# Three edits to the RWKV stage of a fused transformer kernel: V's projection in one run ahead of the scan, a shorter last level of a triangular inverse, and row factors computed earlier

## The reference, cut to what matters

```python
xr = h + hh * mu[0]   # and xw, xk, xv, xa, xg: six mixtures of h and its predecessor
r = xr @ w_r
w = -jax.nn.softplus(-(w0 + jnp.tanh(xw @ w1) @ w2)) - 0.5
k = xk @ w_k
v = xv @ w_v
a = jax.nn.sigmoid(a0 + (xa @ a1) @ a2)
g = jax.nn.sigmoid(xg @ g1) @ g2
kk = k * k_k, normalised per head
k = k * (1.0 + (a - 1.0) * k_a)
def step(state, inp):                      # 256 steps, 16 heads of 64
    sa = jnp.einsum('bhvk,bhk->bhv', state, a_t)          # a_t = -kk
    state = state * w_t + sa * b_t + v_t * k_t            # b_t = kk * a
    y_t = jnp.einsum('bhvk,bhk->bhv', state, r_t)
y = group norm of y, + sum(r * k * r_k) * v, times g, then @ w_o
```

## Time and profile before

| | |
|---|---|
| median of 3 runs | 1463.24 us |
| the profiled execution: its own time, its span | 1461.14 us, 1459.3 us |
| granted TensorE clock, mean over the span | 0.992 |
| busy: TensorE, weight loads, VectorE, ScalarE, GpSimd | 95%, 81%, 61%, 49%, 10% |
| chain that ended last, by engine | TensorE 79%, VectorE 8%, ScalarE 4%, issue 3%, GpSimd 2%, DMA 2% |
| the RWKV layer's projections R to V, start to end | 704.51 to 780.27 us |
| scan, first pass and second pass, start of each | 780.75 and 836.67 us |
| scan's end | 895.61 us |

### The profile page before, as it was taken

How to read it: one execution, slowest core, us unless ns; L and a number is a source line. 1 busy time by engine, 2 the same in 40 slices (tenths; PEclk the granted TensorE clock), 3 DMA queues, 4 the chain that set the end, 5 groups by cost and what they waited for, 6 DMA issues and landing times.

```text
span 1459.3 us, 25739 instructions
## 1 busy us (share of the span) xinstructions
PE 1393.1 (95%) x10574; PEld 1177.2 (81%) x10574; DVE 888.2 (61%) x1230; ACT 720.6 (49%) x988; POOL 144.0 (10%) x143
## 2 busy tenths in 40 slices
PE   8999999999999999999898988999999988899998
PEld 8966988987997998885576767799997765699997
DVE  5665655557476655566957677565456666455553
ACT  5455644446545544445555334454444665354442
POOL 0162011100000101100100102000000223000000
PEclk9999999999999999999999999999999999999999
DMA  8733665555646476555454001456474632165462
GB/s 298 234 108 102 199 201 179 168 187 171 216 147 206 159 220 189 190 170 169 146 141 160 4 4 34 155 179 203 147 236 150 209 104 58 57 217 185 142 222 89
DMA packets 86589, 231.93 MB, mean 159 GB/s; under 512 B 15926, under 2 KB 21702, under 8 KB 86346
## 3 DMA queue, kind: packets, MB, share of 16 engines
q1 hardware_dynamic: 85912, 228.17, 49.1%
q0 software_dynamic: 560, 2.11, 0.4%
HBM read 228.14 MB, written 1.08 MB: 157 GB/s over the span
## 4 chain that ended last, share of the span: by engine, by line
PE 79%; DVE 8%; ACT 4%; issue 3%; POOL 2%; DMA 2%; SPq 0%; DVEq 0%; ACTq 0%; POOLq 0%
PE PS L441 48%; PE PS L444 28%; PE PS L456 3%; ACT SH L413 1%; DVE SL L419 1%; POOL AB L818 1%; DVE AB L792 1%; DVE SL L416 1%; DMA ST<-in_rw_w_o 1%; DMA ST<-in_rw_w_v 0%; POOL SM L886 0%; ACT XH L604 0%; DMA ST<-in_w_ple_gate 0%; DVE X L707 0%; ACT JK L589 0%
## 5 line engine op out<-in xcount | busy, mean ns | idle before, releaser
L419 DVE SCALAR_TENSOR_TENSOR SL<-ST,SM,SH 128x1024 fp32r<-128x1024 f32 (+1 forms) x256 | 315.1, 1249 | 168.9 <-ACT SH L413 128.4
L413 ACT ACTIVATE SH<-ST,SM 128x1024 fp32r<-128x1024 f32 (+1 forms) x256 | 282.4, 1122 | 198.6 <-PE PS L444 124.7
L441 PE MATMUL PS<-XH,SH 128*128 128x256 f32 x1224 | 344.2, 281 | 1.5 <-DVE XL L605 1.5
L444 PE MATMUL PS<-XH,SL 128*128 128x256 f32 x1224 | 344.4, 281 | 0.0
L441 PE MATMUL PS<-XL,SH 128*128 128x256 f32 x1224 | 343.5, 281 | 0.0
L416 DVE TENSOR_TENSOR SL<-ST,SH 128x1024 fp32r<-128x1024 f32 (+1 forms) x153 | 196.6, 1299 | 152.3 <-ACT SH L413 126.4
L441 PE MATMUL PS<-SH,XH 128*128 128x512 f32 x544 | 222.6, 409 | 12.9 <-DVE SM L807 2.6
L441 PEld LDWEIGHTS PS<-XH,SH 128*128 128x128 f32 x1224 | 231.3, 189 | 2.9 <-ACT SH L413 1.7
L413 ACT ACTIVATE SH<-ST 128x1024 fp32r<-128x1024 f32 (+1 forms) x153 | 158.5, 1051 | 147.4 <-PE PS L444 123.9
L441 PEld LDWEIGHTS PS<-XL,SH 128*128 128x128 f32 x1224 | 229.1, 187 | 0.9
L444 PEld LDWEIGHTS PS<-XH,SL 128*128 128x128 f32 x1224 | 229.2, 187 | 0.2
(11 more groups left out here) (317 smaller groups left out, 1458.1 us busy)
## 6 DMA issues: line engine op xcount, KB each, us to landing
ST<-in_ffn_w_gu SPq DMA_DIRECT2D x80, 512.0 KB, 4.7
ST<-in_w_mlp_up SPq DMA_DIRECT2D x64, 512.0 KB, 4.7
ST<-in_w_mlp_down SPq DMA_DIRECT2D x64, 512.0 KB, 4.4
ST<-in_ffn_w_down SPq DMA_DIRECT2D x44, 512.0 KB, 4.3
ST<-in_w_attn_in SPq DMA_DIRECT2D x24, 512.0 KB, 4.9
ST<-in_w_conv_in SPq DMA_DIRECT2D x24, 512.0 KB, 4.5
ST<-in_w_ple_gate SPq DMA_DIRECT2D x16, 512.0 KB, 4.3
ST<-in_kv_w SPq DMA_DIRECT2D x16, 512.0 KB, 4.2
```

What stands on the lines that cost most here:

```text
L413: a = ac.do(lambda e: e.activation(h[p0:p1, 0:cols], t[p0:p1, 0:cols], ACT.Copy, scale=sc), ready, t_gt, pe_done.get(i - NSPLIT))
L419: b = ve.do(lambda e: e.scalar_tensor_tensor(l[p0:p1, 0:cols], t[p0:p1, 0:cols], sc, h[p0:p1, 0:cols].bitcast(F32), ALU.mult, ALU.subtract ...
L441: pe.go(lambda e: e.matmul(o, l, r, start=start, stop=stop, skip_group_check=skip))
L444: return pe.do(lambda e: e.matmul(o, l, r, start=start, stop=stop, skip_group_check=skip))
```

## The change

1. The list of units: the two units of the gate's first factor (g1), one unit of V, the gate's second factor (g2, g2t), and then the other seven of V; before, four of V stood ahead of g1, two between g1 and g2, two behind.
2. The order around R: the decay's `low_rank_out` stands ahead of `mix(3)`; the wait for all four banks ahead of R's first unit is gone (`kind_a` waits bank by bank); the terms from a stand behind R's sixth unit, the triangular sums between its sixth and seventh. The products with R (TT, KN, RN) stand behind the gate's first factor. The four strided reads of PE_ stand right behind the writes that they wait for.
3. Lanes 0 and 1 take banks 4 to 7 and lanes 2 and 3 banks 0 to 3; VN is evacuated half by ScalarE, half by VectorE; the products that read V stand in a part of their own, `inputs`, behind the inverse.
4. The last level of the inverse writes only what it changes: eight products of 64 x 32 into the corner of the transposed matrix, and two copies of 32 partitions each; no addition to XX, no `flip`.
5. `kind_a` calls `early` (in `enter`: `raw_rstd`) behind the splits of its second group, ahead of the splits of the two units after it.

The diff, cut to its core:

```diff
-    eight("rw_w_v_2", range(4))
     tails = set()
     for k in range(2):
         tails.add(len(units))
         unsplit(g1v[:, 4 * k:4 * k + 4, :], 640)
-    eight("rw_w_v_2", range(4, 6))
+    eight("rw_w_v_2", range(1))
     unsplit(A["rw_g2_2"][0][0:128, :])
     special("g2t", 512)
-    eight("rw_w_v_2", range(6, 8))
+    eight("rw_w_v_2", range(1, 8))
...
-            us = take_group(len(g), len(g) - 1 if lead else look)
+            if early is not None and not lead:
+                us = take_group(len(g), len(g) - 1)
+                early()
+                early = None
+                while n_split[0] < min(n_used[0] - len(g) + look + 1, len(units)):
+                    unit_split()
...
-    wait_banks([0, 1, 2, 3])
     pe.wait(m0)
     kind_a(XM[0], range(1), (0, 1, 2, 3), last=False)
...
+    _, t_sg = low_rank_out(LFW, SG, [lfw, one], c)
     m3 = mix(3, 2)
-    _, t_sg = low_rank_out(LFW, SG, [lfw, one], c)
     kind_a(XM[0], range(4, 5), (0, 1, 2, 3), first=False, last=False)
     _, t_ag = low_rank_out(LFA, AG, [lfa, one], m3[4], xg)
-    trr = kind_a(XM[0], range(5, 8), (0, 1, 2, 3), first=False)
-    er = evac_act(RN, (0, 1, 2, 3), trr, xn_free)
+    kind_a(XM[0], range(5, 6), (0, 1, 2, 3), first=False, last=False)
...
+    trr = kind_a(XM[0], range(6, 8), (0, 1, 2, 3), first=False)
+    er = evac_act(RN, (0, 1, 2, 3), trr, xn_free, t_k)
...
-    ev = [ac.do(lambda e, m=m: e.activation(VN[:, m, :], PS[:, m * 1024:m * 1024 + 1024], ACT.Copy), tvv[m]) for m in range(2)]
+    ev = [ac.do(lambda e: e.activation(VN[:, 0, :], PS[:, 0:1024], ACT.Copy), tvv[0]),
+          ve.do(lambda e: e.tensor_copy(VN[:, 1, :], PS[:, 1024:2048]), tvv[1])]
...
-    lane_slots = [(0, 1), (4, 7), (9, 10), (11, 13)]
+    lane_slots = [(0, 1), (11, 13), (4, 7), (9, 10)]
...
-        z.bk = (2 * s, 2 * s + 1)
+        b0 = (4, 6, 0, 2)[s]
+        z.bk = (b0, b0 + 1)
...
+            if n == 4:
+                t = products(z, [(ob(z, m, c * 32, 32, hl), Z[hf(hl), c, m, :], XT[hf(hl), m, c, 32:64]) for m in range(2) for c in range(2) for hl in range(2)])
+                z.xt = []
+                for hl in range(2):
+                    r = slice(64 * hl, 64 * hl + 32)
+                    z.xt.append(ac.do(lambda e, r=r: e.activation(XT[r, :, :, 32:64], two(z, 0, 64)[r].rearrange("p m (c i) -> p m c i", c=2), ACT.Copy), t))
+                free_both(z, z.xt)
+                yield
+                break
...
+        yield from inputs(p, z)
         wait_banks(z.bk)
         pe.wait(z.xt, z.am)
```

More of the change, by code:

```diff
@@ L456, in tr_t, with kind_a @@
         return pe.do(lambda e: e.transpose(o, i, ID))
-    def kind_a(xs, kbs, banks, first=True, last=True, xt=None, end=False, mid=None, look=LOOK):
+    def kind_a(xs, kbs, banks, first=True, last=True, xt=None, end=False, mid=None, look=LOOK, early=None):
         tok = [None, None]
@@ L469, in kind_a @@
             lead = head and g is groups[0]
-            us = take_group(len(g), len(g) - 1 if lead else look)
+            if early is not None and not lead:
[4 more added lines that the diff above has]
+                    unit_split()
+            else:
+                us = take_group(len(g), len(g) - 1 if lead else look)
             for m in range(2):
@@ L664, in second, with early @@
             r[1] = raw_half(1, tb[1])
-        return kind_a(XS[0], range(8), banks, xt=r, mid=second, end=True, **kw)
+        def early():
+            entered.append(raw_rstd())
+        return kind_a(XS[0], range(8), banks, xt=r, mid=second, end=True, early=early, **kw)
     rt_free = [None]
@@ L1516, in emit @@
         bfree[4 + b4] = t_pp
+    trr = kind_a(XM[0], range(6, 8), (0, 1, 2, 3), first=False)
+    er = evac_act(RN, (0, 1, 2, 3), trr, xn_free, t_k)
     scr2 = nc.dram_tensor("scr2", (4, D), F32).ap()
-    t_pe = [dma_once(scr2[2 * m:2 * m + 2, :], PP[63:128:64, m, :], t_pp) for m in range(2)]
+    t_pe1 = [dma_once(scr2[2 * m:2 * m + 2, :], PP[63:128:64, m, :], t_pp) for m in range(2)]
     t_px = [dma_once(PX[64 * c + 1:64 * c + 64, :, :], PP[64 * c:64 * c + 63, :, :], t_pp, trr) for c in range(2)]
[L1520 to L1536, removed]
+    t_px1 = [po.do(lambda e, c=c: e.memset(PX[64 * c:64 * c + 1, :, :], 1.0), trr) for c in range(2)]
+    t_pe = [dma_once(PE_[:, 8 * mc:8 * mc + 8], scr2[mc, :].rearrange("(p f) -> f p", f=128), t_pe1, slow=True) for mc in range(4)]
     pe.wait(xg)
@@ L1552, in emit, with v_units @@
         bfree[4 + o] = gsp[o]
[L1553 to L1557, removed]
+    t_rk = ve.do(lambda e: e.tensor_tensor(TT[:, :, :], RN[:, :, :], KN[:, :, :], ALU.mult), er, t_k, t_cu)
+    tk_ = ve.do(lambda e: e.tensor_tensor(KN[:, :, :], KN[:, :, :], PI[:, :, :], ALU.mult), t_pi, t_rk)
+    tr_ = ve.do(lambda e: e.tensor_tensor(RN[:, :, :], RN[:, :, :], PP[:, :, :], ALU.mult), t_pp, t_rk)
+    tvv = [None, None]
+    def v_units(ks):
+        for k in ks:
+            i, h, l = take()
+            for m in range(2):
+                for n in range(2):
+                    tvv[m] = mm3(bank(2 * m + n), [x[:, k, m * 128:(m + 1) * 128] for x in XM[2]], [x[:, n * 512:(n + 1) * 512] for x in (h, l)], k == 0, k == 7)
+                if m:
+                    pe_done[i] = tvv[m]
+                yield
+    wait_banks([0, 1, 2, 3])
+    pe.wait(m3)
+    for _ in v_units(range(1)):
+        pass
+    ta_ = ve.do(lambda e: e.scalar_tensor_tensor(KK[:, :, :], KK[:, :, :], -1.0, PX[:, :, :], ALU.mult, ALU.mult), t_px, t_px1, t_b)
+    tb_ = ve.do(lambda e: e.tensor_tensor(AG[:, :, :], AG[:, :, :], PI[:, :, :], ALU.mult), t_b, t_pi)
     wait_banks([4, 5, 6, 7])
@@ L1674, in head, with inputs @@
         yield
+    def inputs(p, z):
+        AM, MG = z.AM, z.MG
         wait_banks(z.bk)
@@ L1811, in run, with finish @@
                     gens.remove(g)
-    lw, lwt, lwi = param()
-    lb, lbt, lbi = param()
     y_res = {}
-    def finish(d, toks):
+    ln = []
+    def finish(d):
+        if not ln:
+            ln.extend([param(), param()])
+        (lw, lwt, lwi), (lb, lbt, lbi) = ln
+        toks = [y_tok[2 * d], y_tok[2 * d + 1]]
         def cols(x):
@@ L1857, in emit @@
     run([lane(k, lanes[k]) for k in range(4)])
-    run([lane(4 + k, lanes[k]) for k in range(4)] + [finish(d, y_tok[2 * d:2 * d + 2]) for d in range(2)])
-    scan_done = [[z.fr, z.tail_free] for z in lanes] + [y_tok]
+    run([lane(4 + k, lanes[k]) for k in range(4)] + [finish(d) for d in range(2)])
+    scan_done = [[z.fr, z.tail_free] for z in lanes] + [list(y_tok.values())]
     def block_split(m):
@@ L1889, in emit @@
     res = [block_split(m) for m in range(2)]
-    last = {d: finish(d, y_tok[2 * d:2 * d + 2]) for d in (2, 3)}
+    last = [finish(d) for d in (2, 3)]
     for _ in range(5):
-        for d in (2, 3):
-            next(last[d])
+        for g in last:
+            next(g)
     wait_banks([4, 5, 6, 7])
@@ L1896, in emit @@
     kind_a(XS[0], range(1), (4, 5, 6, 7), last=False)
-    run([last[2]])
+    run(last[:1])
     kind_a(XS[0], range(1, 3), (4, 5, 6, 7), first=False, last=False)
     res = [quarter(2)]
-    run([last[3]])
-    par_done(lwi, list(y_res.values()))
-    par_done(lbi, list(y_res.values()))
+    run(last[1:])
+    for q in ln:
+        par_done(q[2], list(y_res.values()))
     kind_a(XS[0], range(3, 4), (4, 5, 6, 7), first=False, last=False)
```

55 lines of the change are left out of this document (36 added, 19 removed).

## The result

The change made the kernel 4.5 us faster, not 10.4: 1458.44 us in place of 1462.95 (medians of 20 runs each), a ratio of 0.9972 with a 95% interval of 0.9962 to 0.9983. By the bound of 0.5% that is no difference, where faster was forecast. The time lies in the range of 1446 to 1460, with less than half of the forecast gain.

What follows compares the result with a forecast made beforehand. TensorE, busy 95% of the span, was taken as the bound, so only its idle time and slow clock could be won. Terms 4.7 + 1.2 + 1.3 + 2.0 + 0.4 - 0.35 + 1.1 gave 10.4 us: about 1453, range 1446 to 1460.

Steps and rivals of the forecast that it cites:

- The forecast's terms for that stretch: Ahead of the scan: 1.16 us at R's first unit, 4.7 at the low-rank stage, 0.48 at the first transposition.
- the 729.6 worked out: Low-rank stage: time when ScalarE's four g1 copies end, with AGR's two halves behind them, done at 731.5.
- V's run had no gaps: V's units in one run: cost put at nothing; gaps over 1 us between units would show the forecast wrong.
- its wait of 0.84 us: Start of the scan: TensorE's wait for T4's copy before the first product goes, part of a 1.3 us gain.
- `block_split` waits 0.35 us for lane 2's bank: Behind the scan: `block_split` waits for banks 0 and 1, now lane 2's; term -0.35 us (-1 to 0).
- SG at the second embedding stage: SG would wait for TensorE instead of GpSimd and could start 0.9 us sooner.
- the second pass's step: Scan's second pass: start 1.0 us sooner, GpSimd's wait taking the rest; last level costs 0.6; net 0.4 us gain.
- First pass: Scan's first pass: `head` gives back 2.6 us, the inputs return at the last level for 0.6; net 2.0 us gain.
- The early factors: Early row factors at the embedding stages: 0.2 us at the first, 0.9 at the second; term 1.1 us gain.
- Rival 1: The scan gives nothing: narrow copies cost more, GpSimd's powers grow, lanes wait for one another; 1456 us, chance 0.2.
- Rival 2: V's run starves on late loads or VectorE's splits, costing 3 to 6 us; 1457 us, chance 0.1.
- Rival 3: TensorE's clock falls to 1.2 GHz in the scan, up to 19 us more; 1472 us, chance 0.05.

Runs made afterwards that it cites:

- e1: The kernel before with the early row factors alone: 1458.06 us, 0.9978 of before.
- e7: The changed kernel with the KK,CC products done by four VectorE copies a lane: 1454.88 us, 0.9941 of before.
- e10: The changed kernel with inputs in `head`, the old full last level, and ScalarE copies in place of the KK,CC products: 1452.90 us, 0.9936 of before.
- e5: The changed kernel with the KK,CC products of both m joined, 4 in place of 8 a lane: 1455.34 us, 0.9961 of before.
- e8: e7 with the last level made full again (64x64 products, XX, flip): 1457.28 us, 0.9959 of before.

## Why the prediction was wrong

**What held.** From K's evacuation to the scan's first transposition before took 79.1 and 78.7 us (e1 78.9), all kernels with the new front 72.6, but e7 73.2 and e10 73.1: 6.1 to 6.5 us less, 6.3 on average. The forecast's terms for that stretch sum to 1.16 + 4.7 + 0.48 = 6.3. AGR came at 727.3; the 729.6 worked out, less the 2.1 us by which this execution was ahead at K's end, is 727.5. V's run had no gaps. The scan's first product came without its wait of 0.84 us. `block_split` waits 0.35 us for lane 2's bank, as forecast. SG at the second embedding stage waits for TensorE.

TensorE and VectorE in the second pass:

```profile
851.18 0.59 PE L440 MATMUL PS<-Z,XT 64*64 64x64 f32 x11 [2.69 <-DVE Z L1735]
853.70 1.97 PE L455 MATMUL PS<-CC,XX 128*128 128x128 f32 x8 [0.54 <-DVE XX L1752]
```

```profile
849.50 1.28 DVE L1900 TENSOR_TENSOR RN<-RN,PR 128x512 f32<-128x512 f32 x2
850.71 1.41 DVE L1735 TENSOR_TENSOR Z<-PS,CC 128x256 f32<-128x256 f32 x4
```

The powers on GpSimd and the norm's steps on VectorE take back most of `head`'s gain, as the second pass's step said: from `head`'s first transpositions to those of the second level it took 15.5 us before and takes 14.3, 1.2 us less where 1.0 was forecast.

**The step that failed** is the last level in "First pass", which the "Second pass" took over: that the inputs return there at a price of 0.6 us. From the fourth level's transpositions to LG,WZ it took 6.8 us before. Forecast was 7.4, and 10.9 came in the first pass; in the second it was 9.5. The term holds ScalarE's copies alone. The 64 products that return (KK,CC and VN,MG, 256 instructions) stand in it at nothing on TensorE, "since ScalarE ends the round". In the trace ScalarE waits there for TensorE, and TensorE for its instructions. The copies' own miss (0.29 for 0.25 us, eight of them) is only 0.3 us. By its instructions the stretch to TB,QT grows from 1184 to 1424, 0.94 blocks, 3.5 us at 3.7 us a block; measured between the second profiles, 3.6 and 3.1 us. So the two passes together were not 2.4 us shorter, but 2 to 3 longer: the scan takes 118.8 and 120.5 us in the changed kernel, 117.9, 116.7 and 115.6 in the three profiles with the old one. The early factors give 3.2, the front 6.3, the scan with its first wait in it -3.0 (mean 119.7 less 116.7). That is 6.5 us, against a measured 4.5 and 5.2. The 1.3 to 2.0 us left over may be scatter of the terms; I did not place them. The early factors gave 2.1 us more than their term of 1.1, for a reason that is open: by that luck the time missed the forecast by less than the scan did.

The signs were in the trace of before. Its first pass has four pauses with the releaser "issue", 3.7 us in sum, 3.8 and 3.9 us apart at its end. The last three, from the timeline of TensorE:

```profile
820.72 0.38 PE L441 MATMUL PS<-AGR,WZ 64*64 64x64 f32 x9 [0.97 <-issue]
824.55 0.39 PE L444 MATMUL PS<-VN,KN 64*64 64x64 f32 x11 [1.27 <-issue]
828.44 0.40 PE L444 MATMUL PS<-VN,KN 64*64 64x64 f32 x11 [0.87 <-issue]
```

I had passed over them, and let 256 instructions a pass move into that very stretch at no price.

**The rivals.** Rival 1 (the scan gives nothing, 1456) came nearest to what happened, but for another cause than ScalarE and GpSimd. Rival 2 came nearest in time (1457), by luck: V's run did not starve. Rival 3: in the second pass of the changed kernel the clock is at its lower level for some 10 us in the first profile and 7 in the second, before for 7. That is 1.7 us at most, not 19:

```profile
840.00:842.00 2.00, 1.84 (x14) 0.96 (x18) 2.00 (x4) 1.11 (x4) 0.00 (x0) 0.60 0.00 0
850.00:854.00 4.00, 2.29 (x66) 2.09 (x66) 4.00 (x11) 0.00 (x0) 0.00 (x0) 0.58 0.00 0
```

## What to carry to other kernels

Where TensorE runs many small fp32 products, count its instructions as well as its columns: a stretch has a second bound, instructions times the time of a block, and pauses put down to "issue" at even distances say that it is reached. There, work moved in from a stretch with idle time costs its instructions in full, and what helps is fewer instructions: products joined (e5), or plain moves of data given to an engine with time to spare (e7, e10). It is not sure to help: e8 took 112 a pass away, and its median did not move.

## What the runs showed that was not expected

- TensorE's instructions arrive in blocks of 256. In a stream that outruns them a block takes 3.45 to 4.0 us (mean 3.64), with the DMA queues otherwise at rest (busy 2%, 4 to 5 GB/s); a product of fp32 is four instructions (two matmuls, two weight loads), so one product in 57 ns on average.
- The same 64x64 fp32 matmul takes 16 ns when it goes round the four quarters of the array and two banks (128 in 2.1 us), and 58 ns when all use one quarter and one place (1022 in 59.8 us).
- A stretch of 3.4 us at 1.2 GHz comes at the same few places of the program, but not in each execution (near 457 us in six of the 12 profiles). Over the 20 runs of the changed kernel, 9 us from lowest to highest, time and mean clock correlate by -0.85.
